# Moving a residual from the end of a kernel to the change of its two passes, as transposes into accumulators

## What is computed

```python
h = h + mix
h = h + peer_ffn(rmsnorm(h, norm_ffn_w[layer]), w_query[layer], sub_keys[layer],
                 expert_u[layer], expert_v[layer])
...
return (rmsnorm(h, final_norm_w), ...)

# in peer_ffn, for every row x, its 8 heads and 16 experts of each
act = jax.nn.gelu(jnp.einsum('nd,nhed->nhe', xb, u), approximate=False)
return jnp.einsum('nhe,nhed->nd', gb * act, expert_v[eb])
```

## Time and profile before

| | |
|---|---|
| median of three runs | 1844.85 us (1838.57, 1844.85, 1849.69) |
| the profiled execution, its own time | 1842.69 us |
| its span, first to last instruction | 1840.9 us |
| mean granted clock of TensorE | 0.991 |
| PE busy | 1777.0 us (97% of the span), 11497 instructions |
| DVE busy | 1384.3 us (75%) |
| ACT, POOL busy | 712.9 us (39%), 681.8 us (37%) |

### The profile page before, as it was taken

The page is one execution under the profiler, slowest core; times in us unless marked ns, Lnnn a source line. Parts: engine busy times, 40 slices in busy tenths (PEclk is TensorE's granted clock), DMA queues, the critical chain, the costliest instruction groups (busy, mean ns, idle before and its releaser), DMA issues.

```text
span 1840.9 us, 29413 instructions
## 1 busy us (share of the span) xinstructions
PE 1777.0 (97%) x11497; PEld 1728.0 (94%) x11497; DVE 1384.3 (75%) x2533; ACT 712.9 (39%) x1244; POOL 681.8 (37%) x448
## 2 busy tenths in 40 slices
PE   7999987979999999999999999999999999999998
PEld 6998886879999999999999999999999999999997
DVE  4887887674899999999865665437697888887752
ACT  4546325453333334443433333333233333333332
POOL 3000000000004586777876767742353333333100
PEclk9999999999999999999999999999999999999999
DMA  7211101053313688888998989899999999999731
GB/s 215 69 47 43 36 5 49 24 150 124 118 47 111 218 275 264 295 294 311 300 322 293 308 313 318 289 378 354 338 402 374 339 347 361 342 342 355 293 118 38
DMA packets 190706, 424.33 MB, mean 231 GB/s; under 512 B 11162, under 2 KB 119222, under 8 KB 180320
## 3 DMA queue, kind: packets, MB, share of 16 engines
q1 hardware_dynamic: 153256, 287.47, 45.3%
q0 software_dynamic: 37312, 134.97, 20.8%
HBM read 360.76 MB, written 62.06 MB: 230 GB/s over the span
## 4 chain that ended last, share of the span: by engine, by line
PE 75%; DVE 19%; ACT 3%; issue 2%; POOL 1%; DMA 0%; SPq 0%; DVEq 0%; ACTq 0%; POOLq 0%
PE psum L1321 32%; PE psum L1300 21%; PE psum L927 9%; PE psum L1288 3%; PE psum L922 3%; DVE cT L1943 2%; DVE junk L2461 2%; PE psum L1030 2%; PE psum L1078 1%; DVE besti L2336 1%; DVE oh L2451 1%; DVE besti L2324 1%; DVE sring L2328 1%; DVE eqx L2394 1%; DVE pick L2399 1%
## 5 line engine op out<-in xcount | busy, mean ns | idle before, releaser
L1300 PE MATMUL psum<-xT,WS 128*128 128x416 f32 x3072 | 594.8, 353 | 2.8 <-POOL WS L862 2.7
L1321 PE MATMUL psum<-AR,WS 128*128 128x416 f32 x3072 | 582.1, 351 | 2.6 <-DVE AR L2532 2.6
L1321 PEld LDWEIGHTS psum<-AR,WS 128*128 128x128 f32 x3072 | 575.6, 188 | 9.0 <-DVE AR L2532 3.0
L1300 PEld LDWEIGHTS psum<-xT,WS 128*128 128x128 f32 x3072 | 572.2, 188 | 8.5 <-POOL WS L862 4.0
L862 POOL TENSOR_TENSOR WS<-RAWP,WS 128x1024 fp32r<-128x1024 f32 x128 | 310.9, 2439 | 315.6 <-ACT WS L1730 215.0
L853 POOL DMA_INDIRECT rowg<-in_expert_v,idx x128 | 182.0, 1422 | 317.6 <-DVE acc L2475 309.7
L927 PE MATMUL psum<-xT,WR 128*128 128x280 f32 (+2 forms) x1968 | 272.0, 296 | 4.7 <-DVE WR L1830 3.3
L1740 ACT ACTIVATE WS<-RAWP 128x1024 fp32r<-128x1024 f32 x128 | 135.6, 1059 | 336.2 <-PE psum L1321 325.9
L927 PEld LDWEIGHTS psum<-xT,WR 128*128 128x128 f32 x1968 | 258.1, 191 | 6.6 <-DVE WR L1830 3.6
L2525 DVE TENSOR_TENSOR WS<-RAWP,WS 128x1024 fp32r<-128x1024 f32 x128 | 156.5, 1223 | 116.2 <-ACT WS L1740 116.2
L1767 ACT ACTIVATE actA<-psum 128x416 f32<-128x416 f32 x128 | 66.3, 518 | 401.8 <-PE psum L1300 395.5
(11 more groups left out here) (372 smaller groups left out, 1662.0 us busy)
## 6 DMA issues: line engine op xcount, KB each, us to landing
RAWP<-in_expert_u SPq DMA_DIRECT2D x64, 1024.0 KB
RAWP<-in_expert_v SPq DMA_DIRECT2D x64, 1024.0 KB
act_dram<-actA SPq DMA_DIRECT2D x128, 208.0 KB
gate_dram<-gblk SPq DMA_DIRECT2D x26, 1024.0 KB
act<-act_dram SPq DMA_DIRECT2D x64, 416.0 KB
Gt<-gate_dram SPq DMA_DIRECT2D x16, 1664.0 KB
RAW<-in_w_in SPq DMA_DIRECT2D x8, 1024.0 KB, 6.0
RAW<-in_w_query SPq DMA_DIRECT2D x8, 1024.0 KB, 8.0
```

The costliest lines, as they stand in the source:

```text
L1300: last = mm(bank[e % 2][:, 0:TD], ws(e)[:, pw, kt * P:(kt + 1) * P], xT[:, px, kt, TSP:TPE], start=(kt == 0 and i == 0), stop=(kt == KT - ...
L1321: last = mm(bank[dt][:, 0:TD], ws(NK + e)[:, pw, dt * P:(dt + 1) * P], AR[:, e % 4, pa, :], start=(e == 0 and i == 0), stop=(e == NK - 1 a ...
```

## The change

The residual of the dense rows goes into the accumulators before pass 2 adds anything, in their transposed layout. Four DMAs on SP load the four tiles of h during pass 1, at block 100 (`HD_AT`), into `hcols` (the columns of `xT` that only the sparse rows used), `wrow` and `hrest`. Before pass 2 starts, PE multiplies each 104 x 128 piece of h with the identity: 4 tiles for each of the banks 4, 5, 6, 7, 2, 3 stand ahead of the waits of block 0, those of banks 0 and 1 inside block 0. So pass 2 starts no accumulation group any more, it only adds. At the end the eight residual matmuls are gone, and the 32 identity matmuls become 32 plain transposes into banks that need hold nothing. The load of `hf` at block 16 of pass 2 shrinks to tile 0, and the load of the last norm's weights into `wrow` there waits until PE is through with the residual.

```diff
+HD_AT = 100
...
+        hrest = at("hrest", [P, D], F32, used["e"])
+        hcols = at("hcols", [P, 2 * KT, NT], F32, w_xT)
...
-        hf = at("hf", [P, NTP, D], F32, w_xT)
+        hf = at("hf", [P, D], F32, w_xT)
...
+        def dense_rows(t):
+
+            if t <= 2:
+                return hcols[0:DB, KT * (t - 1):KT * t, 0:P]
+            return (wrow if t == 3 else hrest)[0:DB, :].rearrange("p (k n) -> p k n", k=KT)
...
+                if e == HD_AT:
+                    V.wait(sp, "pairs", ND)
+                    sp.wait_ge(h2_done, 32)
+                    for t in range(1, NTP):
+                        sp.dma_start(dense_rows(t), h2_dram[t, 0:DB, :].rearrange("p (k n) -> p k n", k=KT)
+                                     ).then_inc(hd_in, 16)
...
                     sp.wait_ge(s_mm, NK)
+                    T.wait(sp, "hT")
                     load_row(final_norm_w.rearrange("(a d) -> a d", a=1), row_in[2])
-                    sp.dma_start(hf[:, 0, :], h2_dram[0]).then_inc(hf_in, 16)
-                    sp.dma_start(hf[0:DB, 1:NTP, :], h2_dram[1:NTP, 0:DB, :].rearrange("t p d -> p t d")
-                                 ).then_inc(hf_in, 16)
+                    sp.dma_start(hf[:], h2_dram[0]).then_inc(hf_in, 16)
...
+            def residual(dt):
+
+                if dt == 4:
+                    pe.wait_ge(hd_in, 64)
+                    pe.wait_ge(gate_bank, 2 * NBAT)
+                    V.wait(pe, "pairs", ND)
+                elif dt == 2:
+                    pe.wait_ge(dot_done, PAIRS)
+                elif dt == 0:
+                    pe.wait_ge(gelu_done, NK)
+                for t in range(1, NTP):
+                    last = mm(bank[dt][:, (t - 1) * DB:t * DB], dense_rows(t)[:, dt, :], ident[0:DB, 0:DB],
+                              start=(t == 1), stop=False)
+                return last
+
+            for dt in (4, 5, 6, 7, 2, 3):
+                residual(dt)
             for e in range(NK):
...
-                    if e == 0:
-                        if dt == 4:
-                            pe.wait_ge(gate_bank, 2 * NBAT)
-                            V.wait(pe, "pairs", ND)
-                        elif dt == 2:
-                            pe.wait_ge(dot_done, PAIRS)
-                        elif dt == 0:
-                            pe.wait_ge(gelu_done, NK)
+                    if e == 0 and dt < 2:
+                        T.op(residual(dt), "hT")
...
-                                  start=(e == 0 and i == 0), stop=(e == NK - 1 and i == 2))
+                                  start=False, stop=(e == NK - 1 and i == 2))
...
-            pe.wait_ge(hf_in, 32)
             for d in range(KT):
-                t, i = 1 + d // 2, d % 2
                 (A if d % 2 else V).wait(pe, "yT", d)
-                mm(bank[d][0:DB, :], ident[0:DB, 0:DB], hf[0:DB, t, 512 * i:512 * i + 512], start=True, stop=False)
             for t in range(1, NTP):
                 for j in range(KT):
-                    last = mm(psum[0:DB, 1024 * (t - 1) + j * P:1024 * (t - 1) + (j + 1) * P],
-                              yT[:, j, (t - 1) * DB:t * DB], ident[:], start=False, stop=j % 4 == 3)
+                    last = pe.transpose(psum[0:DB, 1024 * (t - 1) + j * P:1024 * (t - 1) + (j + 1) * P],
+                                        yT[:, j, (t - 1) * DB:t * DB], ident[:])
```

More of the change, by code:

```diff
@@ L365, in build @@
         sq2 = at("sq2", [P, D], F32, w_rowg + 2 * D)
-        assert used["e"] <= room - D
+        hrest = at("hrest", [P, D], F32, used["e"])
+        hcols = at("hcols", [P, 2 * KT, NT], F32, w_xT)
+        assert used["e"] + D <= room - D and P <= TSP
         yoT = at("yoT", [P, 3, D], F32, w_Gt)
-        hf = at("hf", [P, NTP, D], F32, w_xT)
-        yT = at("yT", [P, KT, TD], F32, w_xT + NTP * D)
-        assert NTP * D + KT * TD <= 2 * KT * NT
+        hf = at("hf", [P, D], F32, w_xT)
+        yT = at("yT", [P, KT, TD], F32, w_xT + D)
+        assert D + KT * TD <= 2 * KT * NT
         psum = ctx.enter_context(nc.psum_tensor("psum", [P, 8 * 512], F32))
@@ L407, in build @@
         hf_in = sem("hf_in")
+        hd_in = sem("hd_in")
         y_out = [sem(f"y_out{i}") for i in range(2)]
@@ L1797, in _ @@
                     V.wait(act, "hf", 0)
-                    fn(yo[:, 1, :], hf[:, 0, :], ACT.Square, "ss", 3, 0, accum_out=fs[:, 0:1])
+                    fn(yo[:, 1, :], hf[:], ACT.Square, "ss", 3, 0, accum_out=fs[:, 0:1])
                 if e == AX_END + 8:
@@ L2534, in _ @@
                     dve.wait_ge(axpy_done, PAIRS)
-                    dve.wait_ge(hf_in, 32)
-                    op(tt(hf[:, 0, :], hf[:, 0, :], acc[:], ALU.add), "hf", 0)
+                    dve.wait_ge(hf_in, 16)
+                    op(tt(hf[:], hf[:], acc[:], ALU.add), "hf", 0)
                 if e == AX_END + 6:
@@ L2543, in _ @@
                     chain(dve.reciprocal(fs[:, 8:9], fs[:, 16:17]))
-                    op(dve.scalar_tensor_tensor(yo[:, 0, :], hf[:, 0, :], fs[:, 8:9], wrow[:], ALU.mult, ALU.mult),
+                    op(dve.scalar_tensor_tensor(yo[:, 0, :], hf[:], fs[:, 8:9], wrow[:], ALU.mult, ALU.mult),
                        "yo", 0)
```

## The result

The changed kernel took 1833.16 us in the median of 19 runs (1831.22 to 1837.90), the kernel before 1844.52 (1836.49 to 1852.82). The ratio is 0.9942, with a 95% interval of 0.9930 to 0.9954: 10.7 us or 0.6% faster, and more than twice the 3.9 us that the sum had given. The profiled execution took 1833.46 us, its span is 1831.7 us against 1840.9.

The account below looks back on a forecast made before the run. PE was taken to bound the kernel, busy for 97% of the span. -6.85 us at the end and +2.9 at the pass change (7.1 - 2.6 - 1.6) sum to -3.9 us; forecast 1840.0 us, range 1834 to 1846.5.

Parts of the forecast that it names:

- the sum: Whole kernel: -6.85 us at the end plus 2.9 us at the pass change gives -3.9 us.
- The end: After pass 2: tile 1 ready and ACT starting 6.85 us earlier, the 1.81 us train of later tiles unchanged.
- rival (c): At the end: transposes run one behind another at full duration, 0.27 us; saving only 1.5 us, 1842.4; chance 0.08.
- The residual: At the pass change: 32 matmuls, 64 instructions at 111 ns each, cost 7.1 us.
- Given back at the pass change: Between passes: PE's 2.6 us of idle time vanish, and the clock no longer falls, worth 1.6 us.
- (a): Behind the pass change: the clock falls all the same, 1.6 us not got back; -2.3 us, 1841.6; chance 0.12.
- (b): At the pass change: the residual runs at half clock, 222 ns an instruction; +3.1 us, about 1847; chance 0.08.
- From then on PE never waits: Pass 2 before the change: 3072 matmuls in 581.7 us, one every 189 ns, so time added earlier delays the end.
- What costs nothing. The loads: Moving 1.7 MB from block 16 of pass 2 to block 100 of pass 1, near 1068 us, costs nothing.
- one of the prediction's own signs of being wrong: In pass 1: PE idles from 1068 us on where it did not before.
- rival (d): In pass 1: the moved loads disturb gathers or pairs, up to 4 us; sum near 0, 1844; chance 0.05.
- the range: Whole kernel: 1834 to 1846.5 us, from the lowest and highest run less 3.9 us and a little for (b).

Follow-up runs that it names:

- end only: The kernel before with only the new end: no residual matmuls, 32 plain transposes, dense rows' residual left out; 0.9955 of before.
- break: The kernel before with one small fp32 matmul into unused columns between blocks 3 and 4 of pass 2; 1.0012 of before.
- load spread: The kernel before with the 1.7 MB load at block 16 of pass 2 cut into four, at blocks 36 to 84; 0.9981 of before.
- before again: The kernel before, unchanged, profiled a second time on another chip; 0.9992 of before.
- filler: The kernel before with 24 matmuls of the residual's form, results overwritten, put ahead of block 0 of pass 2; 0.9998 of before.
- load back: The changed kernel with 1.7 MB of rows that nobody uses loaded at block 16 of pass 2 again; 0.9980 of before.
- mixed: The changed kernel with the residual of tiles 1 to 3 as fp32 transposes, tile 4 still an fp32 matmul; 0.9912 of before.

## Why the prediction was wrong

Its terms for the end and for the pass change held. The number that it took for the cost of one pass-2 matmul did not, and neither did its account of the loads.

- **The end: -6.85 us.** Right. 6.86 us between the profiles and 6.84 with the end alone. The first tile was ready as worked out, the transposes stood 109 ns apart (rival (c) did not come), and the train of 1.8 us a tile was unchanged.
- **The residual: +7.1 us at 111 ns.** Right. The first 48 took 5.27 us (1236.72 to 1241.99), 110 ns each. Four moving columns took 111 to 115 ns and 104 take 110, so the moving columns do not set this pace. That the weight load does is not shown: as transposes the same pieces, with the same 128 weight columns, stood 89 ns apart.
- **Given back at the pass change: -2.6 and -1.6 us.** The idle time went. The half clock went too, but it was a matter of chance in before: of the five profiles with that gap and nothing put behind it ahead of block 0's own work it is in three (before, end only, break) and not in two (load spread, before again). Rivals (a) and (b) did not come: the clock stayed at 1.00 over 64 small matmuls.
- **"From then on PE never waits: 3072 matmuls in 581.7 us, one every 189 ns."** This is the step that failed. The 189 ns were read as what such a matmul costs. They were one of two rhythms, and the stop at the pass change (the gap, or in before the gap with the half clock behind it) had set it. Filling the gap was worth 6.8 us more than the idle time and the half clock together. The earlier trace rows hold what could have raised the question: a stop at the start of the stream; what they do not show is the fast rhythm, which in before lasts for three distances ahead of the clock's fall (182, 188 and 190 ns), or how long the same matmuls take in it: 127 blocks at 4480 ns instead of 4533.
- **"What costs nothing. The loads", where they had been.** Wrong: I did not ask what the load disturbed there. DVE waited 9.1 us for activations; the page of before shows it. In the slow rhythm (before twice, end only) DVE waits 8.3 to 9.6 us and PE just escapes. In the fast one, with the load at block 16 (filler, break, load back), DVE waits 11.7 to 12.7 us and PE stands still, and the stall would have taken back most of the gain: 7 us when the load was put back.
- **"What costs nothing. The loads", where they went.** Wrong too. SP issues them behind block 100, from 1101.71 us on and not near 1068, and there the DMA share of before is 0.92 and 1.10, not the 0.58 of the earlier trace rows. The gate store behind them was issued at 1107.11 us and landed 17 us later (in before again, without the loads, 9 us), and ACT waited for it (us in total, times, longest, from 1105 to 1140 us):

```profile
ACT gblk L1805 <- DMA gate_dram<-gblk: 6.4, 1, 6.4
```

In the two profiles of the changed kernel this wait, 6.4 and 5.8 us, stayed off PE. In the other five with these loads it was 9.8 to 11.6 us and PE idled for 1.6 to 3.3 us in pass 1, one of the prediction's own signs of being wrong. It is rival (d) in another form: the gates come late, not the gathers or pairs. What it costs the executions without a profile is not known. A gate store issued ahead of the four loads was not tried.

- **The sum** then is -6.85 + 2.9 - 6.8 = -10.8 us, the ratio of the times gives -10.7, and the two traces from the last start of pass 1 on give -11.0. The lower end of the range was one low run of before less 3.9 us, and had no case in it in which a term was missing.

## What to carry to other kernels

When two profiles of a PE-bound stream are both 100% busy at full clock, compare the distance between the starts of the same matmuls, not the busy time: a stream may run in more than one steady rhythm (here there were two), and a stop anywhere in it can cost its whole rest. A short idle gap at the head of a long stream is then worth more than its length; work that fits into it, or one small fp32 matmul behind it, is a cheap thing to try, although in the break kernel alone the matmul gained nothing, because the late activations stopped PE again. And when a large load moves, read what waited near its old place as well as near its new one, and ask whether a faster stream would now run into it. At the new place look at what stands behind it in the same queue: here it was a store that another engine waits for.

## What the runs showed of the hardware

- Matmuls of one form (128 x 128 weights, 416 moving columns, full clock) ran 186.7 or 188.9 ns apart on average, in patterns that repeat every three, for up to 575 us. One fp32 matmul of 32 columns turned slow into fast, in the kernel before and in the changed one; idle time of 1.8 to 3 us turned fast into slow in four places, in three of them with half clock behind it and in one (load back) without. Why there are two, and what in PE holds the one or the other, stays open; so does the exception in the mixed kernel.
- Idle time of 2.6 us with the same work around it was followed by half clock in some executions and not in others.
- A load of 1.7 MB, where the DMA share was 0.9 and more already, held up what was issued behind it: with it at block 16 of pass 2 DVE waited 8.3 to 12.7 us for activations in six profiles, and with it at block 100 of pass 1 a gate store took 17 to 21 us to land instead of 9.
- 32 fp32 transposes in a row at the end of the changed kernel ran 109 ns apart at a granted clock of 1.00. The Trainium skill (TensorE: Matmul & The Clock Gate, Part 4: PE-mode transpose) gives about 275 ns for a 128 x 128 bf16 transpose in one kernel's context. The duration of a single fp32 one here, about 0.27 us, is near that figure; the distance between two in a row is not.
